# The union of the stages' buffers placed behind the matmuls' inputs in SBUF, in a six-block transformer kernel on one core

## The reference, cut to what matters

```
def first_block(x, c, positions, ...):
    for l in range(2):
        x = x + gate1 * token_mixing(x, ...)       # one wide projection, four branches, an output projection
        x = x + gate2 * channel_mixing(x, ...)

def channel_mixing(x, shift, scale, g_pre, w_up, ffn_conv, w_down, g_post):
    h = rmsnorm(x, g_pre) * (1.0 + scale) + shift
    a, b = jnp.split(h @ w_up, 2, axis=-1)         # w_up: 1024 x 5632
    y = (jax.nn.silu(causal_dwconv(a, ffn_conv)) * b) @ w_down
    return rmsnorm(y, g_post)

def swiglu(x, w_gu, w_down):
    g, u = jnp.split(x @ w_gu, 2, axis=-1)         # w_gu: 1024 x 5632, w_down: 2816 x 1024
    return (jax.nn.silu(g) * u) @ w_down

def second_block(x, p, norm_gains, ...):
    for layer in range(4):
        h = x + 0.5 * swiglu(rmsnorm_2(x, g[0]), w_ffn_gu[layer, 0], w_ffn_down[layer, 0])
        h = h + mixer(rmsnorm_2(h, g[1]))          # hgrn2, mlstm, sliding window attention, hgrn2
        h = h + 0.5 * swiglu(rmsnorm_2(h, g[2]), w_ffn_gu[layer, 1], w_ffn_down[layer, 1])
        gate = jax.nn.sigmoid(rmsnorm_2(h, g[3]) @ w_ple_gate[layer])
        x = h + gate * (p[layer] @ w_ple_proj[layer])
```

## Time and profile before

| | us |
|---|---|
| median of 3 runs | 3467.45 (3466.78 to 3470.16) |
| the profiled execution | 3468.48 |
| its span | 3466.7 |
| TensorE busy (matmuls) | 3254.7, 94% |
| VectorE busy | 2475.9, 71% |
| ScalarE busy | 1762.6, 51% |
| GpSimd busy | 3.0 |

### The profile page before, as it was taken

The page is one execution under the profiler, slowest core; times in us unless marked ns, Lnnn a source line. Parts: engine busy times, 40 slices in busy tenths (PEclk is TensorE's granted clock), DMA queues, the critical chain, the costliest instruction groups (busy, mean ns, idle before and its releaser), DMA issues.

```text
span 3466.7 us, 64588 instructions
## 1 busy us (share of the span) xinstructions
PE 3254.7 (94%) x27162; PEld 3153.1 (91%) x27162; DVE 2475.9 (71%) x3728; ACT 1762.6 (51%) x2673; POOL 3.0 (0%) x6
## 2 busy tenths in 40 slices
PE   6899899999999999979999998999999999998998
PEld 6789899988989899879999978999989999987998
DVE  8987798887667766876575666667576667688665
ACT  4555444455454545664454445455455455457444
POOL 0000000000000000000000000000000000000000
PEclk8899999989999999989999999999999999998999
DMA  8445487434546455425545433554533554542453
GB/s 304 144 170 200 163 308 286 151 125 140 177 158 225 158 184 183 153 74 198 187 166 186 174 122 131 188 183 171 184 133 137 183 183 171 188 165 87 161 186 112
DMA packets 163920, 597.93 MB, mean 172 GB/s; under 512 B 18192, under 2 KB 18224, under 8 KB 163376
## 3 DMA queue, kind: packets, MB, share of 16 engines
q1 hardware_dynamic: 163632, 593.81, 48.8%
HBM read 592.69 MB, written 1.05 MB: 171 GB/s over the span
## 4 chain that ended last, share of the span: by engine, by line
PE 80%; DVE 14%; ACT 4%; issue 2%; DMA 1%; SPq 0%; DVEq 0%; ACTq 0%
PE ps L451 25%; PE ps L452 25%; PE ps L453 25%; DVE wlo L415 4%; DVE fa L1520 1%; ACT whi L403 1%; PE ps L1112 1%; DVE hl L1737 1%; DVE land L526 0%; PE ps L654 0%; PE ps L1228 0%; DVE tmps L559 0%; DMA land<-w_ada 0%; DMA land<-w_in 0%; DVE tmps L557 0%
## 5 line engine op out<-in xcount | busy, mean ns | idle before, releaser
L451 PE MATMUL ps<-hh,whi 128*128 128x256 f32 x5472 | 1547.5, 283 | 59.5 <-DVE hl L1737 27.2
L452 PE MATMUL ps<-hl,whi 128*128 128x256 f32 x5472 | 1539.6, 281 | 0.0
L453 PE MATMUL ps<-hh,wlo 128*128 128x256 f32 x5472 | 1535.2, 281 | 0.0
L415 DVE TENSOR_TENSOR wlo<-land,whi 128x1024 fp32r<-128x1024 f32 (+1 forms) x1032 | 1217.5, 1216 | 224.1 <-ACT whi L403 223.3
L403 ACT ACTIVATE whi<-land 128x1024 fp32r<-128x1024 f32 (+1 forms) x1032 | 1028.2, 1044 | 171.8 <-PE ps L453 157.2
L451 PEld LDWEIGHTS ps<-hh,whi 128*128 128x128 f32 x5472 | 1037.5, 190 | 67.9 <-issue 50.4
L452 PEld LDWEIGHTS ps<-hl,whi 128*128 128x128 f32 x5472 | 1037.6, 190 | 0.6
L453 PEld LDWEIGHTS ps<-hh,wlo 128*128 128x128 f32 x5472 | 1037.5, 190 | 0.0
L451 PE MATMUL ps<-ra,whi 128*128 128x256 f32 (+1 forms) x2416 | 691.0, 286 | 20.9 <-DVE ra L1428 10.4
L453 PE MATMUL ps<-ra,wlo 128*128 128x256 f32 (+1 forms) x2416 | 688.0, 285 | 0.0
L452 PE MATMUL ps<-ra,whi 128*128 128x256 f32 (+1 forms) x2416 | 686.9, 284 | 0.0
(11 more groups left out here) (415 smaller groups left out, 2427.4 us busy)
## 6 DMA issues: line engine op xcount, KB each, us to landing
land<-w_gu SPq DMA_DIRECT2D x352, 512.0 KB, 3.5
land<-w_dn SPq DMA_DIRECT2D x176, 512.0 KB, 3.6
land<-w_in SPq DMA_DIRECT2D x136, 512.0 KB, 3.5
land<-w_ada SPq DMA_DIRECT2D x96, 512.0 KB, 3.8
land<-w_up SPq DMA_DIRECT2D x88, 512.0 KB, 4.1
land<-hg_in SPq DMA_DIRECT2D x64, 512.0 KB, 3.5
land<-w_down SPq DMA_DIRECT2D x44, 512.0 KB, 4.5
land<-ple_gate SPq DMA_DIRECT2D x32, 512.0 KB, 3.5
```

Source lines behind the costliest of these rows:

```text
L415: dve.tensor_tensor(w.lo, g.slot(n), w.hi.bitcast(F32), ALU.subtract).then_inc(*D_("w_lo", n))
L451: pe.matmul(out, w.hi, x.hi, start=first, stop=False, skip_group_check=skip)
L452: pe.matmul(out, w.hi, x.lo, start=False, stop=False, skip_group_check=skip)
L453: return pe.matmul(out, w.lo, x.hi, start=False, stop=last, skip_group_check=skip)
```

## The change

The five requests for `ra1`, `fa1`, `crow`, `ra2` and `fa2` move from the end of `Program.__init__` to just behind `hl`. `ra2` and `fa2` are no longer given back, so that what follows lies behind them; they hold 19,200 columns, `ra1`, `fa1` and `crow` 19,072.

```diff
         self.hh = sb("hh", NC * T, F32R)
         self.hl = sb("hl", NC * T, F32R)
         self.h = Pair(self.hh, self.hl)
+        with ExitStack() as inner:
+            self.ra1 = inner.enter_context(nc.sbuf_tensor("ra1", [128, 6656], F32R))
+            self.fa1 = inner.enter_context(nc.sbuf_tensor("fa1", [128, 11392], F32))
+            self.crow = inner.enter_context(nc.sbuf_tensor("crow", [128, TILE], F32))
+        self.ra2 = sb("ra2", 4096, F32R)
+        self.fa2 = sb("fa2", 15104)
         self.par = sb("par", NPAR)
         self.con = sb("con", NCON)
         self.attn = sb("attn", 1152)
@@
         self.ps = [ctx.enter_context(nc.psum_tensor(f"ps{i}", [128, 512], F32)) for i in range(8)]
-        with ExitStack() as inner:
-            self.ra1 = inner.enter_context(nc.sbuf_tensor("ra1", [128, 6656], F32R))
-            self.fa1 = inner.enter_context(nc.sbuf_tensor("fa1", [128, 11392], F32))
-            self.crow = inner.enter_context(nc.sbuf_tensor("crow", [128, TILE], F32))
-        with ExitStack() as inner:
-            self.ra2 = inner.enter_context(nc.sbuf_tensor("ra2", [128, 4096], F32R))
-            self.fa2 = inner.enter_context(nc.sbuf_tensor("fa2", [128, 15104], F32))
```

## The result

The changed kernel takes 3447.99 us (median of 6 runs, 3444.81 to 3452.03), the kernel before 3468.92 us beside it (6 runs). The ratio is 0.994, with a 95% interval from 0.9928 to 0.9953: 21 us, 0.6%, faster. The profiled execution took 3448.35 us, against 3468.48; its span is 3446.6 us.

A forecast was written before the change was run, and what follows sets the result against it. It took TensorE, busy 94% and mostly on mm3's matmuls, as the bound. Savings of 17.4 + 3.2 + 1.7 + 7.4 less 3.5 and 0.5 gave 25.7 us off, so 3443 us, range 3434 to 3461.

The forecast's parts named there:

- the leading case: Matmul stream of mm3: with one residue for all it keeps its starting pace, mostly 116.7 ns; 3443 us, chance 0.50.
- the mixed paces: Rival, mm3: hh stays as mixed between 116.7 and 117.8 ns as before and ra follows; 3450 us, chance 0.23.
- What bounds the kernel, and where the 3 ns come from: TensorE's mm3 lines: ra takes 120.0 ns against 116.7 or 117.8 for hh, because of where ra lies.
- `par` to `causal`, `fa`, `crow`: cost 0: Other moved buffers: par to causal keep their residues, fa and crow go from 480 to 160; cost 0.
- The pace: Feed-forward streams: one residue keeps the starting pace; hh blocks now at 117.8 save 7.4 us, less 3.5 for two stages.
- The sum over the feed-forward stages: Ten feed-forward stages: ra saves 17.4 us, hh blocks behind ra 7.4, less 3.5 for two slow stages.
- The other parts: ra matmuls outside feed-forward: projections save 3.2 us, mixing stages 1.7, counting half of the latter's 1008 matmuls.
- What would show it: Signs: ra rows at or under 281 ns, 48 in 5.60 to 5.66 us, cycles of 16.80 us in most feed-forward stages.
- No effect: Rival: the place isn't the cause, something else that goes with ra is; 3467 us, chance 0.10.
- half the effect: Rival: residues matter but so do other address bits, ra gains half, some 12 us; 3455 us, chance 0.08.
- slower: Rival: writes to ra's neighbours slow it, and hl beside ra would pay 15.3 us instead; 3483 us, chance 0.04.
- all falls into 117.8: Rival, mm3: ra saves 14.8 us, hh matmuls now at 116.7 lose 8.8, 6.0 in all; 3461 us, chance 0.05.

The follow-up runs named there:

- d3_dist_288_480: Changed kernel with more padding, putting hh and hl at distance 288 and ra at 480 from their weights modulo 512; 3449.68 us, ratio 0.995.
- f2_dist_32_192: Changed kernel with 160 unused bytes ahead of the union, hh and hl staying at distance 32, ra at 192; 3436.07 us, ratio 0.9903, two runs.
- g1_changed_again: The changed kernel run again without any edit; 3446.27 us over 4 runs, ratio 0.9935 against the kernel before.
- e1_old_place_160: Kernel before with 192 unused bytes ahead of the union, shifting ra, fa and crow to 160 modulo 512 in their old place; 3443.87 us, ratio 0.9931.
- e2_new_place_480: Changed kernel with 320 unused bytes ahead of the union and 192 behind, ra, fa and crow at 480 modulo 512; 3470.65 us, ratio 1.001.
- h1_all_at_192: Changed kernel with 192 instead of 32 unused bytes between weights and x, putting hh, hl and ra at distance 192; 3443.87 us, ratio 0.9922.

## Why the prediction was right, point by point

It gave 3443 us, a range of 3434 to 3461, and faster at 0.81; 3448 came out. The time alone doesn't speak for the leading case: its rival, the mixed paces, gave 3450, which is nearer. The cycles decide between them.

- **What bounds the kernel, and where the 3 ns come from.** Right, and shown: the same `ra` matmuls go from 120.0 to 116.7 ns by a shift of 192 bytes in the old place, and back by one of 320 in the new place. Since these shifts change nothing but addresses, the other engines, the accumulators and the array are not what makes the difference, as I had argued from the rows of before. I also called what lies over 106.7 ns a cost of the operands' delivery; no run shows that. What was left open there, distance or own residue, is settled for distance. I said that bits over 512 seem not to count; by the pairs of distances 256 bytes more don't either.
- **`par` to `causal`, `fa`, `crow`: cost 0.** Right within what can be seen: L1427 425 ns after 425, L1803 418 after 419.
- **The pace.** Right, and the step on which most hung. I said that a stream keeps the pace that it starts with if no block of another distance throws it out, and that 16.80 us would be the cycle of most feed-forward stages: it was in seven of eight in the second block, 16.96 in the eighth. The two of the first block changed pace in their course, each at a place where two starts lie further apart (0.16 and 0.23 us). In both profiles of the changed kernel none of the runs of over 200 matmuls with all starts within 0.15 us, the longest of 1583, changed between 116.7 and 117.8. Not every other distance throws a stream out, though: counted along the timelines, a block of `hh` behind one of `ra` was at 117.8 in 67 of 99 cases before, but its blocks at 288 in `d3_dist_288_480` (`ra` at 480) in 4 of 99, and those at 32 in `f2_dist_32_192` (`ra` at 192) in none of 99. I took off 3.5 us for two bad stages; one whole and two in part came, which is near that by luck, since `g1_changed_again` had two whole and one in part.
- **The sum over the feed-forward stages.** 17.4 + 7.4 - 3.5 = 21.3 us expected, 22.7 measured in the first profile, 19.8 in the second.
- **The other parts.** The term that was mis-sized: 3.2 + 1.7 = 4.9 us expected, a loss of 2.6 measured in the first profile and a gain of 4.8 in the second. The matmuls did get cheaper: 129 of `ml_out` take 15.05 us (the line below, 116.7 ns each), where 129 of `hg_out` took 15.48 before. But the clock stood at 0.50 for 15 us more in the first profile and for 3 us less in the second. A matmul takes 0.21 us at that clock and 0.117 at the full one, so by an estimate 15 us there cost some 7. That is as much as the 6.5 us (1968 x 3.3 ns) that the `ra` matmuls outside of the feed-forward stages can give at most, and would account for the loss. I had named the drops as "a few us either way, inside" and given them no width of their own.

```profile
2098.51:2113.56 15.05, 15.05 (x130) 15.05 (x130) 3.27 (x6) 8.28 (x11) 0.00 (x0) 1.00 0.35 125
```

- **What would show it.** The blocks and cycles came as named. The mean durations came out at 284 and 282 ns instead of 281 or less: the same rows of `hh` have 283 and 281, so a mean over all of a kernel, with its starts behind gaps and its half-speed stretches, can't be compared with 281 that closely.
- **The rivals.** The paces of `hh` as mixed as before, the likeliest of them, is refuted by the cycles: seven stages keep 16.80 us throughout. No effect, half the effect and slower fell with `e1_old_place_160` and `e2_new_place_480`. That all falls into 117.8 happened not here but in seven stages of `h1_all_at_192`. What it would have cost here was not run.

## What to carry to other kernels

When the same matmul form has two start-to-start times in one trace, sort them by operand and write down where the operands begin modulo 256 bytes: here the distance between the moving operand and the weights made up to 6.7 ns of 120, and a pad of a few columns was the whole edit. Try several distances on the chip, since neither "equal" nor "near" was best, and judge each by long stretches of start-to-start time, not by mean durations. Look also at whether the pace is the same all through a stream, for a layout can have a fast and a slow one, and a trial of one block beside others doesn't tell what a whole stream will do.

## What the runs showed that I had not expected

- The pace belongs to the stream and not to the single matmul. At distance 32 it is 116.7 or 117.8 ns, at 192 it is 113.3 or 117.8, at 16 there are three. Distance 32 has a third pace too, that of `ra` before: the line below, from the changed kernel, is 168 `hh`/`hl` matmuls of the second mixing stage at 120.0 ns, and `g1_changed_again` has one run of 143 like it. What picks one at a start stays open: the changed kernel had its slow stage in `ha2` in one profile and in `ha3` in another.

```profile
951.62:971.78 20.16, 20.16 (x169) 20.16 (x169) 11.22 (x12) 10.65 (x12) 0.00 (x0) 1.00 0.56 208
```

- A mix of distances may be better than the best distance alone. `f2_dist_32_192` had the lowest ratio of all, 0.9903, but from two runs, and its interval (0.9867 to 0.9939) overlaps with those of the changed kernel and of `h1_all_at_192`. That it beats both is likely from its ten feed-forward stages, which sum up to 1896.6 us against 1912.8 in the changed kernel and 1913.2 in `h1_all_at_192`, and not settled by its times.
- In some executions the granted clock stays at 0.50 for 58 us in the mixer `mx2`, after and before stretches at 1.00, and costs 17 us, nearly as much as the whole change brings.
- Why the distance matters was not taken apart. That two reads of TensorE, the weights of the next matmul and the moving operand of this one, get in each other's way would fit that only their distance counts and that `hh` and `ra` take the same 0.21 us at the lower clock, but no run here separates the two reads.
